# Two half reciprocals and eight spreading products in every norm of a two-block transformer kernel

## The reference, cut to what matters

```
def _rmsnorm(x, g):
    xf = x.astype(jnp.float32)
    y = xf * lax.rsqrt(jnp.mean(xf * xf, axis=-1, keepdims=True) + NORM_EPS)
    return (y * g.astype(jnp.float32)).astype(x.dtype)

f = _swiglu(_rmsnorm(x, ffn1_pre_g), ...)          # n1
x = x + 0.5 * _rmsnorm(f, ffn1_post_g)             # p1
h = _rmsnorm(x, mix_pre_g)                         # n2
...
x = x + _rmsnorm(merged @ w_out, mix_post_g)       # p2
f = _swiglu(_rmsnorm(x, ffn2_pre_g), ...)          # n3
x = x + 0.5 * _rmsnorm(f, ffn2_post_g)             # p4
# second block, for l in 0, 1:
h = _rms_norm(x, norm1_g[l]) * (1.0 + sc1) + sh1   # l1
...
h = _rms_norm(x, norm2_g[l]) * (1.0 + sc2) + sh2   # l2
```

## Time and profile before

| | us |
|---|---|
| median of 3 runs | 2676.03 |
| lowest, highest | 2673.92, 2678.38 |
| profiled execution | 2673.17 |
| its span | 2671.4 |
| PE busy in it | 2580.1 (97%) |
| DVE, ACT, POOL busy | 1111.3, 1027.5, 1082.5 |

### The profile page before, as it was taken

The page is one execution under the profiler, slowest core; times in us unless marked ns, Lnnn a source line. Parts: engine busy times, 40 slices in busy tenths (PEclk is TensorE's granted clock), DMA queues, the critical chain, the costliest instruction groups (busy, mean ns, idle before and its releaser), DMA issues.

```text
span 2671.4 us, 40390 instructions
## 1 busy us (share of the span) xinstructions
PE 2580.1 (97%) x16848; PEld 2099.4 (79%) x16848; DVE 1111.3 (42%) x1739; ACT 1027.5 (38%) x1590; POOL 1082.5 (41%) x586
## 2 busy tenths in 40 slices
PE   8999989999998999997999999999999999999999
PEld 6888867787886888885779678888877787788887
DVE  4666131314333666304654634441037555343310
ACT  4223242526333322224533744443254346544421
POOL 3444443344444444443322244444433313344443
PEclk9999999999999999998999899999999999999999
DMA  5555433121232555432210023222332100222222
GB/s 189 189 192 194 147 114 134 72 89 35 95 106 89 183 192 190 149 100 93 82 64 4 2 79 101 97 95 95 101 118 79 49 3 22 82 95 97 99 95 89
DMA packets 78310, 273.99 MB, mean 103 GB/s; under 512 B 8753, under 2 KB 9521, under 8 KB 78001
## 3 DMA queue, kind: packets, MB, share of 16 engines
q1 hardware_dynamic: 78128, 271.40, 29.9%
HBM read 269.27 MB, written 2.10 MB: 102 GB/s over the span
## 4 chain that ended last, share of the span: by engine, by line
PE 93%; DVE 3%; ACT 2%; issue 1%; POOL 0%; DVEq 0%; PEldq 0%; POOLq 0%; ACTq 0%
PE bank L245 25%; PE bank L247 25%; PE bank L246 25%; PE bank L1640 4%; PE bank L1891 3%; PE bank L888 1%; PE bank L1914 1%; PE bank L890 1%; PE bank L889 1%; PE bank L556 1%; PE bank L1493 1%; PE bank L790 1%; PE bank L543 1%; PE bank L527 1%; PE bank L792 1%
## 5 line engine op out<-in xcount | busy, mean ns | idle before, releaser
L229 POOL TENSOR_TENSOR w_lo<-raw,w_hi 128x1024 fp32r<-128x1024 f32 (+2 forms) x406 | 948.9, 2337 | 1291.7 <-PE bank L247 995.6
L245 PE MATMUL bank<-h_hi,w_hi 128*128 128x512 f32 x2112 | 836.6, 396 | 36.6 <-POOL w_lo L229 12.9
L246 PE MATMUL bank<-h_lo,w_hi 128*128 128x512 f32 x2112 | 827.0, 392 | 0.0
L247 PE MATMUL bank<-h_hi,w_lo 128*128 128x512 f32 x2112 | 826.5, 391 | 0.0
L220 ACT ACTIVATE w_hi<-raw 128x1024 fp32r<-128x1024 f32 x408 | 426.5, 1052 | 530.7 <-PE bank L247 433.6
L245 PEld LDWEIGHTS bank<-h_hi,w_hi 128*128 128x128 f32 x2112 | 398.7, 189 | 142.1 <-issue 47.1
L247 PEld LDWEIGHTS bank<-h_hi,w_lo 128*128 128x128 f32 x2112 | 399.5, 189 | 84.4
L246 PEld LDWEIGHTS bank<-h_lo,w_hi 128*128 128x128 f32 x2112 | 399.8, 189 | 80.0 <-issue 0.5
L245 PE MATMUL bank<-hidden_hi,w_hi 128*128 128x512 f32 x704 | 273.9, 389 | 0.0
L246 PE MATMUL bank<-hidden_lo,w_hi 128*128 128x512 f32 x704 | 273.9, 389 | 0.0
L247 PE MATMUL bank<-hidden_hi,w_lo 128*128 128x512 f32 x704 | 273.9, 389 | 0.0
(11 more groups left out here) (419 smaller groups left out, 2901.2 us busy)
## 6 DMA issues: line engine op xcount, KB each, us to landing
ada<-in_ada SPq DMA_DIRECT2D x96, 512.0 KB, 3.6
raw<-in_ff_up SPq DMA_DIRECT2D x88, 512.0 KB, 5.5
raw<-in_l.ff_up SPq DMA_DIRECT2D x88, 512.0 KB, 3.3
raw<-in_l_fm SPq DMA_DIRECT2D x36, 512.0 KB, 3.3
raw<-in_ff_down SPq DMA_DIRECT2D x32, 512.0 KB, 4.9
raw<-in_l.ff_down SPq DMA_DIRECT2D x32, 512.0 KB, 3.3
raw<-in_l_wo SPq DMA_DIRECT2D x16, 512.0 KB, 3.3
raw<-in_ff_down SPq DMA_DIRECT2D x16, 384.0 KB, 3.2
```

The lines of the kernel that those rows point to most:

```text
L229: pool.tensor_tensor(self.wlo[lo][:, 0:kt * P], self.raw[slot][:, 0:kt * P], self.whi[slot][:, 0:kt * P].bitcast(F32), ALU.subtract).then_ ...
L245: pe.matmul(bank[:, :], wh[:, b], hi[:, k, :], start=first, stop=False)
L246: pe.matmul(bank[:, :], wh[:, b], lo[:, k, :], start=False, stop=False)
L247: return pe.matmul(bank[:, :], wl[:, b], hi[:, k, :], start=False, stop=last)
```

## The change

The reciprocal of 128 columns becomes two of 64 columns, each with a mark of its own (`rows0`, `rows1`). The spread becomes two rounds of four products of 64 columns; each round waits for its half, and writes 64 of the 128 columns of each quarter in bank 6. `rstd` is marked behind the last of the eight. All ten norms go through these two functions.

```
     def spread_pe(self, pe, nm):
         m = self.m
-        pe.wait_ge(*m.done(f"{nm}.rows"))
-        for t in range(NT):
-            row = self.ident[:, 32 * t:32 * t + 1].to_broadcast([P, P])
-            x = pe.matmul(by_time(self.bank[6], t), row, self.tmp[3][:, 0:P], start=True, stop=True)
+        for half in range(2):
+            pe.wait_ge(*m.done(f"{nm}.rows{half}"))
+            for t in range(NT):
+                row = self.ident[:, 32 * t:32 * t + 1].to_broadcast([P, P])
+                at = t * P + half * HD
+                x = pe.matmul(self.bank[6][:, at:at + HD], row, self.tmp[3][:, half * HD:half * HD + HD], start=True, stop=True)
         x.then_inc(*m.mark("pe", f"{nm}.rstd"))
 
     def rms_dve(self, dve, nm):
         m = self.m
         dve.wait_ge(*m.done(f"{nm}.std"))
-        dve.reciprocal(self.tmp[3][:, 0:P], self.tmp[2][:, 0:P]).then_inc(*m.mark("dve", f"{nm}.rows"))
+        for half in range(2):
+            part = slice(half * HD, half * HD + HD)
+            dve.reciprocal(self.tmp[3][:, part], self.tmp[2][:, part]).then_inc(*m.mark("dve", f"{nm}.rows{half}"))
         dve.wait_ge(*m.done(f"{nm}.rstd"))
```

## The result

| | before | changed |
|---|---|---|
| median, us | 2677.23 (8 runs, 2673.92 to 2678.89) | 2683.64 (8 runs, 2681.20 to 2687.63) |
| profiled execution, us | 2673.17 | 2685.28 |
| its span, us | 2671.4 | 2683.5 |
| mean granted clock of PE | 0.983 | 0.980 |

The ratio is 1.0026, 95% interval 1.0015 to 1.0037: slower by 6.4 us in the medians (3.9 to 9.9 by the interval); the forecast was +6.5.

What follows compares the result with a forecast made beforehand. TensorE, busy 97% of the span, was taken to bound the kernel. Six norms awaiting the reciprocal +2.65, one at half clock +1.2, three in streams +2.67: +6.5 us, 2682.6 on the median's footing; 8-in-10 range 2677.5 to 2687.0.

Steps and rivals of the forecast that it cites:

- The bound: Whole kernel: TensorE busy 97% of the span and 93% of the chain; changes count where the chain leaves it or its work grows.
- Part 1: DVE reciprocal in two: 553 ns per half, first half 0.40 us earlier, second ending 1.11 us after the first's start.
- Part 2: Spread, eight products for four: sixteen records for eight, 0.112 us apart as before, set by the weight load.
- The shorter end: Last record of the spread: 64 columns last 218 ns against 275 for 128, so 0.06 us less.
- Part 3: Second half's first weight load waits for the second reciprocal: hidden with 0.33 us to spare, cost 0.
- One open norm: A norm where TensorE waits for the reciprocal, at full clock: +0.44 us; six of them +2.65.
- The seventh: l1 of layer 0, at granted clock 0.50: eight more records 1.70 us, less earlier start and shorter end, +1.2 us.
- The stream norms: n1, n2, n3, spread between chunks of a busy TensorE: eight more records each, 3 x 0.89 = +2.67 us.
- Rival A: Spread: moving columns set the pace, 0.056 us a record; total -2.1 us, 2673.9; chance 0.08.
- B: n1, n2, n3: slack behind them absorbs the added records' cost; total +3.9 us, 2679.9; chance 0.14.
- C: Half-clock stretches next to the norms move: two more +9.9 us, 2686.0; two less +3.1, 2679.1; chance 0.20.
- the sum theory: Theory for the experiments: each spread record costs its 128-column weight load, 0.11 us, whatever its moving columns; the terms add up.

Runs made afterwards that it cites:

- stream norms only: Split reciprocal and products only in n1, n2, n3, the other seven norms as in the kernel before: 2679.36 us, ratio 1.0011.
- open norms only: Split only in the seven norms where TensorE waits for the reciprocal; n1, n2, n3 as in the kernel before: 2680.61 us, ratio 1.0019.
- half reciprocals only: Against the kernel before: two half reciprocals in every norm, four whole 128-column products behind the second: 2675.33 us, ratio 0.9998.
- eight products only: Against the kernel before: one whole reciprocal in every norm, then eight products of 64 columns in two rounds: 2688.73 us, ratio 1.0047.

## Why the prediction was right

- **The bound.** A change counts where the chain leaves TensorE or where TensorE gets more to do: that held, each term stands in the distances between norms.
- **Part 1, the half reciprocal** (553 ns forecast): 553 for the first. The pair ends 0.96 after its start, not 1.11: my line counted the fixed part twice. Hidden either way; the cover was 0.5 us, not 0.33.
- **Part 2, the spacing** (0.112 forecast, by columns 0.056): 0.111. The choice rested on line 429 with two moving columns; the kernels with 32 moving columns and with 64 weight columns show the cause that I took from it. The choice of row mattered more than I said: the earlier trace rows show loads of the first half of the line's sixteen. The other eight read every fourth column of the factor as weights (`by_class`) and stand (1.95 - 0.33)/7 = 0.231 us apart at granted clock 1.00, in the kernel before:

```profile
425.01 1.95 PEld L429 LDWEIGHTS bank<-matrices,mix_factor 128*128 128x128 f32 x8
```

So 128 weight columns are 0.11 us only as they are read in the other eight and in the spread; why this reading takes twice as long, no run tests.
- **The shorter end** (0.06 us): 2.01 us for sixteen in the chain is 1.17 + 8 x 0.111 - 0.05. But the row of a 64-column record says 275 ns, not 218; the record starts sooner behind its load instead (0.05 us against 0.11). That the size came out was luck.
- **Part 3, the wait:** nothing, as forecast; no idle time stands between the halves.
- **One open norm** +0.44: 2.65 against 2.20. **The seventh** +1.2: 4.32 against 3.12. **The stream norms** 0.89: 0.90 at n2.
- **Rival A** is out by the spacing, **B** by the kernel with the stream part alone. **C**, the half-clock stretches, is real and was priced too low for a single execution: in the profiled pair it is some 4.7 of 12.1 us. In the medians of eight runs little of it is left, if the terms hold there as in the trace. The changed kernel's runs show it too: the three under 2682 us have mean clocks of 0.981 to 0.983, the three over 2685 have 0.977 to 0.980.
- **Luck.** The mechanism and its terms are shown, but the agreement of 6.4 with 6.5 is closer than the runs allow: the interval is 3.9 to 9.9, the means differ by 6.9, and the two parts measured alone add up to 7.2 by the medians.
- **Slips** that change nothing: the 218 ns of the earlier trace rows, called a load under rival A, are of a matmul record; 24 records of 0.23 are 5.5 us, not 5.4; rival A would already decide at a pitch under 0.07 us, as 0.56 us between first load and second reciprocal hold eight records.

How far the clock goes with the rest can be seen over the profiled executions, taking the sum theory's term off each span:

| kernel | span | term | span less term | mean clock |
|---|---|---|---|---|
| before | 2671.4 | 0 | 2671.4 | 0.983 |
| stream norms only | 2674.5 | 2.7 | 2671.8 | 0.982 |
| open norms only | 2678.0 | 3.9 | 2674.1 | 0.981 |
| changed | 2683.5 | 6.5 | 2677.0 | 0.980 |
| half reciprocals only | 2676.7 | 0.1 | 2676.6 | 0.979 |
| eight products only | 2687.6 | 9.3 | 2678.3 | 0.978 |

What the records don't explain follows the clock. The kernel with 32 moving columns fits (2685.2 at 0.974), and so does the one with whole products on two row tiles (2673.6 at 0.981). It isn't exact: the kernel with 64 weight columns has 0.982 and lies 17 us above the kernel before, of which its records account for some 9. What remains of that one is open. Open too is whether the split itself makes half-clock stretches more frequent: the half reciprocals alone have 0.979 in their profile and no longer spread, and 112.8 us at clock 0.50 against the 105.8 of the changed kernel, so one execution each can't tell.

## What to carry to other kernels

Before cutting a product into narrower ones to start it sooner, look up what sets its spacing: find a row with the same weights, read in the same way, and few moving columns. If the spacing there is that of the wide product, the weight load sets it, and each cut costs a full load per piece; the start gained must be worth more than all the loads added. And the last piece, the one behind the last input, then takes as long as a whole product with those loads would have, so even a first piece that is fully hidden gains next to nothing (1.76 us against 1.77 on two row tiles). If small products wait for their loads, put them on different row tiles (each with a bank of its own, as here; one bank for both was not run) where the array would be idle afterwards anyway, and leave them on the full array inside a dense stream.

## What the runs showed of the hardware that I had not expected

- Two DVE reciprocals of 64 columns, one behind the other, take 0.96 us together, one of 128 columns 0.95, though a lone one of 64 lasts 0.553: back to back on separate columns the fixed part is paid about once.
- Going from a smaller array tile back to 128 x 128 costs time at the first full record: 0.20 us behind 64 rows (0.43 in the chain for 0.23), and as much behind 64 weight columns, of which 0.06 stand behind the changed kernel's spread too.
- Loads of 128 weight columns stand 0.11 us apart when the columns lie side by side or are one column read 128 times, and 0.23 apart when every fourth column is read (line 429, clock 1.00).
- Where a half-clock stretch begins, against a spread at the same place, changes from one execution to the next, and not with the spread's length alone. At l1 of layer 1 it began 1.5 us after the end of the spread in the kernel before; 0.6 us into it in the changed kernel (3.16 us for 2.0); 0.2 us before it with the half reciprocals and the old products (2.09 for 1.17).
